# Weight slots 64 bytes off the grid of the activations, and a mask that is built later

## What is computed

```python
h = rms_norm(x, attn_norm_w);  proj = h @ w_in
x = x + concat(rwkv7_mixer(proj[:, :3360]), gdn_mixer(proj[:, 3360:])) @ w_out
h = rms_norm(x, ffn_norm_w)
x = x + (silu(h @ ffn_w_gate) * (h @ ffn_w_up)) @ ffn_w_down
x = rms_norm(x, final_norm_w)
# second block
a = rms_norm_2(x, mix_norm_2);  q, k, v, f = split(a @ fox_w_in_2)
s = q k / sqrt(128) + (cum_f[query] - cum_f[key])      # causal, softmax over keys
x = x + (softmax(s) v) @ fox_w_out_2
up = rms_norm_2(x, ffn_norm_2) @ ffn_w_up_2;  gate, val = split(conv3(up))
y = x + (silu(gate) * val) @ ffn_w_down_2
```

## Time and profile before

| what | before |
|---|---|
| median of 2 runs | 2872.76 us |
| profiled execution, its own time | 2874.73 us |
| its span | 2873.0 us |
| its mean granted TensorE clock | 0.961 |
| TensorE busy | 2739.4 us (95%) |
| VectorE busy | 1497.5 us (52%) |
| ScalarE busy | 1108.8 us (39%) |
| GpSimd busy | 63.2 us (2%) |

### The profile page before, as it was taken

How to read it: one execution, slowest core, us unless ns; L and a number is a source line. 1 busy time by engine, 2 the same in 40 slices (tenths; PEclk the granted TensorE clock), 3 DMA queues, 4 the chain that set the end, 5 groups by cost and what they waited for, 6 DMA issues and landing times.

```text
span 2873.0 us, 57087 instructions
## 1 busy us (share of the span) xinstructions
PE 2739.4 (95%) x24185; PEld 2661.3 (93%) x24185; DVE 1497.5 (52%) x1679; ACT 1108.8 (39%) x1050; POOL 63.2 (2%) x69
## 2 busy tenths in 40 slices
PE   7999978788999999999999799998999999999999
PEld 6999778487999999999999799977999999999999
DVE  5457556474454444444344544546456666565443
ACT  3333323232344444343333433434344445454332
POOL 1000130000000000000000000000000000000000
PEclk8999989688999999999999899988999999999999
DMA  5555200001545555555554355520545555555554
GB/s 167 181 185 180 73 3 4 1 1 59 176 148 189 176 188 176 187 178 186 180 180 153 123 188 177 188 88 16 183 153 176 189 176 188 177 186 179 184 182 146
DMA packets 169215, 421.74 MB, mean 147 GB/s; under 512 B 17463, under 2 KB 22140, under 8 KB 168860
## 3 DMA queue, kind: packets, MB, share of 16 engines
q1 hardware_dynamic: 168699, 419.13, 44.8%
q10 hardware_dynamic: 416, 1.18, 0.1%
HBM read 418.16 MB, written 2.10 MB: 146 GB/s over the span
## 4 chain that ended last, share of the span: by engine, by line
PE 89%; DVE 8%; ACT 2%; issue 1%; SPq 0%; DMA 0%; DVEq 0%; POOL 0%; ACTq 0%; POOLq 0%
PE ps L1575 26%; PE ps L1577 26%; PE ps L1576 26%; DVE LOW L874 1%; PE ps L1615 1%; PE ps L1995 1%; DVE NSQ L908 1%; PE ps L1672 1%; ACT HIW L503 1%; PE ps L1699 1%; PE ps L1665 1%; PE ps L1709 1%; PE ps L1728 1%; PE ps L1706 0%; PE ps L1963 0%
## 5 line engine op out<-in xcount | busy, mean ns | idle before, releaser
L874 DVE TENSOR_TENSOR LOW<-RAW,HIW 128x2048 fp32r<-128x2048 f32 (+2 forms) x400 | 910.9, 2277 | 1123.6 <-ACT HIW L503 1123.2
L1575 PE MATMUL ps<-H,HIW 128*128 128x256 f32 x4928 | 1403.1, 285 | 40.8 <-DVE LOW L874 18.9
L1576 PE MATMUL ps<-H,HIW 128*128 128x256 f32 x4928 | 1400.9, 284 | 0.0
L1577 PE MATMUL ps<-H,LOW 128*128 128x256 f32 x4928 | 1400.5, 284 | 0.0
L503 ACT ACTIVATE HIW<-RAW 128x2048 fp32r<-128x2048 f32 (+2 forms) x400 | 758.4, 1897 | 1306.3 <-PE ps L1577 1306.2
L1575 PEld LDWEIGHTS ps<-H,HIW 128*128 128x128 f32 x4928 | 952.9, 193 | 44.8 <-issue 26.1
L1576 PEld LDWEIGHTS ps<-H,HIW 128*128 128x128 f32 x4928 | 953.0, 193 | 0.0
L1577 PEld LDWEIGHTS ps<-H,LOW 128*128 128x128 f32 x4928 | 952.7, 193 | 0.0
L1575 PE MATMUL ps<-HID,HIW 128*128 (+1 forms) x1408 | 398.6, 283 | 0.6 <-DVE LOW L874 0.6
L1576 PE MATMUL ps<-HID,HIW 128*128 (+1 forms) x1408 | 398.5, 283 | 0.0
L1577 PE MATMUL ps<-HID,LOW 128*128 (+1 forms) x1408 | 398.4, 283 | 0.0
(11 more groups left out here) (351 smaller groups left out, 1797.3 us busy)
## 6 DMA issues: line engine op xcount, KB each, us to landing
RAW<-in_ffn_w_up SPq DMA_DIRECT2D x264, 512.0 KB, 4.4
RAW<-in_ffn_w_down SPq DMA_DIRECT2D x176, 512.0 KB, 4.6
RAW<-in_w_in SPq DMA_DIRECT2D x96, 512.0 KB, 4.1
RAW<-in_fox_w_in SPq DMA_DIRECT2D x96, 512.0 KB, 4.3
RAW<-in_ffn_w_gate SPq DMA_DIRECT2D x88, 512.0 KB, 3.8
RAW<-in_w_out SPq DMA_DIRECT2D x32, 512.0 KB, 4.9
RAW<-in_fox_w_out SPq DMA_DIRECT2D x32, 512.0 KB, 4.9
RAW<-in_w_in SPq DMA_DIRECT2D x4, 576.0 KB, 4.9
```

Of the source, the lines that this page charges most:

```text
L874: V.tensor_tensor(LOW[:, u_const % 4, 0:n], RAW[:, u_const % 4, 0:n], HIW[:, u_const % 2, 0:n].bitcast(F32), ALU.subtract).then_inc(lo_mad ...
L1575: mm(o_, hi_w, h_hi, start=start, stop=False)
L1576: mm(o_, hi_w, h_lo, start=False, stop=False)
L1577: i = mm(o_, lo_w, h_hi, start=False, stop=stop)
```

## The change

RAW, LOW, HIW and what the mixers keep at w0 move up by 64 bytes. H, HID and everything behind them move up by 1024 bytes, so they stay on multiples of 1024. The room for this comes from `causal`, which loses its own 512 bytes and takes the place of `upper`. Since `upper` is read until the mixers end, GpSimd now builds `causal` after its mixer work, behind a wait for `weights_place_free`, and raises a new mark, `causal_made`; VectorE waits for that mark once, before the attention's forget bias. No instruction that computes is added or left out.

```diff
-        w0 = o
-        RAW = at("RAW", [P, RAW_SLOTS, UNIT], o)
-        LOW = at("LOW", [P, RAW_SLOTS, UNIT], o, F32R); o += 32768
-        HIW = at("HIW", [P, HI_SLOTS, UNIT], o, F32R); o += 16384
+        w0 = o + 64
+        RAW = at("RAW", [P, RAW_SLOTS, UNIT], w0)
+        LOW = at("LOW", [P, RAW_SLOTS, UNIT], w0, F32R); o += 32768
+        HIW = at("HIW", [P, HI_SLOTS, UNIT], o + 64, F32R); o += 16384
+        o += 1024
         h0 = o
...
-        causal = at("causal", [P, P], r2 + 102208 + 768)
-        masks = r2 + 102208 + 1280
+        masks = r2 + 102208 + 768
+        causal = at("causal", [P, P], masks)
...
-            tick(nc.gpsimd.memset(causal[:], 0.0), "pool_step")
...
-            sel(causal[:], [[-1, P]], 0, 1, fill=-1e30)
             pool.sem_inc(S("masks_made"), 1)
...
+            pool.wait_ge(S("weights_place_free"), 1)
+            tick(nc.gpsimd.memset(causal[:], 0.0), "pool_step")
+            own(pool, "pool_step")
+            sel(causal[:], [[-1, P]], 0, 1, fill=-1e30)
+            pool.sem_inc(S("causal_made"), 1)
...
+            dve.wait_ge(S("causal_made"), 1)
             for i in range(8):
                 got("forget_rows")
```

More of the change, by code:

```diff
@@ L137, in build @@
         chunk_go = at("chunk_go", [P, T], masks + 4096)
-        assert h0 % 1024 == 0 and masks + 5120 <= end and r2 + 90112 + 16600 <= end, (r2, masks, end)
+        assert masks + 5120 <= end and r2 + 90112 + 16600 <= end, (r2, masks, end)
         XIN = at("XIN", [P, NT, D], r2)
```

## The result

The changed kernel takes **2757.98 us** (median of two runs, 2752.03 and 2763.92) against 2872.76: a ratio of 0.960, 95% interval 0.951 to 0.969. That ratio leaves out the longest of the six, which lies more than 1.5% above the shortest and so counts as a slow run; over all six it is 0.968. The prediction was 5.4% faster, 2717 us, with a range of 2700 to 2885 that takes in 2757.98.

A forecast was written before the change was run, and what follows sets the result against it. The prediction took the pace of TensorE's 19,008 weight-stream matmuls to bound the kernel. From a span of 2873.0 us it took 156 us for the faster pace and nothing else, giving 2717 us, 5.4% faster, range 2700 to 2885.

The forecast's parts named there:

- The bound: Whole kernel: the pace of 19,008 weight-stream matmuls on TensorE carries the time; a nanosecond on each is worth 19 us.
- An excess that appears in both ... looks like two reads that get in each other's way.: Weight stream at full clock: stream and load limits both some 8 ns high, inferred to be reads hindering each other.
- If the collisions go, the weight load is the next limit: 111.7 ns. I take this value.: Weight stream: pace falls from 120 to 111.7 ns, taken from plain fp32 line 1699; about 18,800 matmuls, 156 us saved.
- the two limits, 117.5 for the stream and 120 for the load: Weight stream at full clock: 117.5 ns needed with weights already there, 120 ns needed by the weight load.
- Nothing booked for what is late next: ScalarE and VectorE beside the stream: 1.1 us of cover per unit of 5.36 us, tightest in second feed-forward; 0 us.
- The mask at nothing: GpSimd's two mask steps move to the mixers' end, with over 70 us of cover there; 0 us.
- Mixer tiles at nothing: Mixer tiles in the weight slots move 64 bytes; products at lines 1699 and 1909 run alike, near 112 ns; 0 us.
- rival C: Weight stream: the shift makes the weight load meet the stream more often; 3029 us if the excess doubled; chance 0.16.
- B: Weight stream: pace stays at 120 ns, the excess belonging to this kind of matmul; 2865 to 2880 us; chance 0.32.
- near 112 ns: Sign in a feed-forward stretch at clock 1.00: distance between matmul starts, with a unit of 48 near 5.4 us.
- Case A: Weight stream: collisions, mostly removed by the shift; chance 0.52, of which 0.13 for 113 to 117 ns, up to 2815 us.
- its likeliest case: Weight stream at a pace of 111 to 113 ns: 2717 us, own range 2700 to 2745; chance 0.35.

The follow-up runs named there:

- the six: Six more runs of the changed kernel with no edit: median 2783.58 us (2759.15 to 2801.12), ratio 0.967; the longest, 2801.12 us, was profiled.
- the first trace: Profiled execution of the changed kernel in its first measurement, against the kernel before: 2763.92 us.
- 113.3 ns throughout: RAW and LOW moved to 192 bytes and HIW to 320, against the changed kernel's 64 for all: 2753.28 us over five runs, ratio 0.959.

## Why the prediction was right, and where its size was off

**The bound.** Right. The gain is the pace of the stream: it gives 114.5 us, new waiting takes 2.9 back, and the two profiled executions differ by 110.8.

**"An excess that appears in both ... looks like two reads that get in each other's way."** Right in what it claimed of addresses: with the same instructions the pace is 120 ns at distances 0 and 256, wherever the weights themselves lie, and 113.3 at 64. That reads collide is still an inference; the runs show only that the distance sets the pace.

**"If the collisions go, the weight load is the next limit: 111.7 ns. I take this value."** This is the term that was mis-sized, twice. The faster pace is 113.3 ns, 1.6 more than the row of plain fp32 from which it was taken: 18,800 x 1.6 = 30 us of the 156. And the 64 bytes do not remove the rest everywhere: 2427 distances at 117.8 cost 10.8 us in the first trace, 10,695 cost 47.5 in the other. With 120 - 113.91 in place of 120 - 111.7, the step gives 18,800 x 6.09 = 114 us in place of 156. The row was the nearest in kind, but it was a load for another kind of matmul; whether the missing 1.6 ns are the float32r load itself or a last bit of hindrance, no run told. Nor did a run part the two limits, 117.5 for the stream and 120 for the load, from which the step set out. That one shift could give two paces, drawn anew at each stall, was in none of the cases.

**Nothing booked for what is late next.** Right to 3 us. Low halves that TensorE waited for went from 19.5 to 22.4 us, and at 113.3 ns throughout to 22.6: the cover of ScalarE and VectorE held with a unit of 48 x 113.3 = 5.44 us. The share of the DMA engines rose to 0.60 in the second feed-forward, as worked out, and landing from 4.4 to 4.5 us:

```profile
2120.00:2700.00 580.00, 580.00 (x5120) 580.00 (x5119) 356.90 (x375) 272.53 (x224) 0.00 (x0) 1.00 0.60 193
```

**The mask at nothing.** Right: alone it gave a ratio of 1.0001.

**Mixer tiles at nothing.** Right: 111.6 and 112 ns, as before. Line 1909, on which that step and the case against rival C lean, was a product at distance 64 (modulo 256) already and ran like the aligned ones: that plain fp32 shows no dependence on the distance stood in those rows, and it does not carry over to the weight stream.

**The rivals.** B, an unchanged pace, fell with the change, and its best argument, that the aligned fp32 products of line 1699 show no excess, did not carry over to float32r. The rule that stood behind it (the Trainium skill, TensorE: Matmul & The Clock Gate, "Step-by-step: what each phase is for": two independent read ports, so that the load of the next weights takes nothing from the running matmul) does not cover this stream: if the two took nothing from each other, it should not matter where one lies against the other, but moving only the weights against the activations took 120 ns to 113.3, and moving both together left it at 120. The measurement decides; how the two hinder each other no run shows. C, a slower pace, was seen at none of the seven distances; 160 bytes, with no gain, came nearest.

**What the trace was to show.** Starts "near 112 ns" came out at 113.3 and 117.8; the mean told A from B at a glance, as foreseen. Case A's part of 113 to 117 ns, which had a chance of 0.13, is the one that came. That the measured time lies inside the range says little by itself, since 2700 to 2885 us also took in no change at all; what the prediction had right is the cause and the direction, and its likeliest case, 2700 to 2745, did not come.

## What to carry to other kernels

Where the weight load and the stream run side by side and the starts lie further apart than the columns alone need, try the distance between the two tiles modulo 256 bytes; it costs a few bytes of room and was worth 2.5 to 4.2% here, but some distances give nothing. This was seen on float32r products of 256 columns; the plain fp32 products of line 1909 kept 112 ns at distance 64 and at 0. Look at the pace piece by piece between stalls, and run the kernel several times: a mean over a trace, or one lucky run, hides a stream that settles anew after each stall. If the same offset gives two paces, give the loads of a group different distances and see whether the slower one goes.

## What the runs showed of the hardware that was not expected

- Two steady paces of one instruction sequence at one granted clock, 113.3 and 117.8 ns, chosen when the stream starts after a stall and kept for up to 6239 products.
- A pattern that came back at 256 bytes of distance: 113.3 ns was seen at 64 and 192 alone, the lowest median at 64, and no gain at 0 and 160.
- When two of three products streamed 128 columns and not 256, the granted clock stayed at 0.50 for most of a span of 4594 us (0.545 in the mean, one run), and the kernel took 1.6 times as long with less to compute.
